# ScalarE normalises the odd head of each attention pair, and VectorE takes more of the prompt's rows beside it

## The chip, the cores and the metric

The kernel runs on one core of one Trainium2 chip. The metric is device time in microseconds (us) of one execution of the whole program. The core has TensorE (PE in the profile; its weight loads are PEld), VectorE (DVE), ScalarE (ACT), GpSimd (POOL) and SyncE (SP, whose queue starts most DMAs). Each engine works through its own instructions in the order in which they were written, and waits on semaphores for the others.

## The reference, cut to what matters

One encoder layer is applied to a prompt of 256 tokens and to a sample of 512 tokens. The change touches the self-attention of both, and moves work of the prompt's expert layer (`e_down[idx]` against the token) in time.

```python
N_HEADS, N_KV_HEADS, HEAD_DIM = 16, 4, 64

def block_attention(q, k, v):            # without a mask, over all S tokens
    ...
    s = jnp.einsum('bkgqd,bskd->bkgqs', q_blk, k).astype(jnp.float32) * scale
    p = jax.nn.softmax(s, axis=-1).astype(v.dtype)
    return jnp.einsum('bkgqs,bskd->bkgqd', p, v)

def peer_ffn(h, w_q, sub_k1, sub_k2, e_down, e_up):
    ...                                   # 8 heads x 16 experts for each token
    act = jax.nn.gelu(jnp.einsum('nhkd,nd->nhk', e_down[idx], xb))
    return jnp.einsum('nhk,nhkd->nd', g * act, e_up[idx])
```

## The kernel before, in words

The program handles the prompt first (2 tiles of 128 tokens), then the sample (4 tiles): projections of the mixer, self-attention, the mixer's outputs, cross-attention, the choice of experts (routing). After both come the experts. One block holds all stages up to the experts, so each engine runs from one stage into the next; what is shared between stages is handed over by semaphores.

**Self-attention** (`self_attention`) works on pairs of heads. A unit p is one pair of heads (even e = 0, odd e = 1) for one tile of 128 queries: N = 16 units for the prompt with w = 256 keys, N = 32 for the sample with w = 512. Each engine runs the same loop over steps, software-pipelined, and these are the instructions of step s:

- TensorE: `scores(s)` into `lin` (four banks, two per unit, so units s and s-2 share theirs); `turn(s-2)`, which transposes the normalised probabilities of both heads into two more banks of `lin`; `values(s-3)`, which multiplies the transposed probabilities by V into `tr`. `turn(p)` waits until both heads of p are normalised and until `copy` of unit p-1 has emptied the bank (`copied`).
- ScalarE: after every nt units (the last tile of a pair of heads) `T_hi <- tr` (L1000), then `copy(s-3)` (L992, two copies from PSUM into `att_probsT`), then `exp(s)` (L983, two exponentials with the bias `att_nmx` and the sum of each row, `att_rs`). `exp(s)` waits for the maxima of unit s.
- VectorE: `T_lo <- tr - T_hi` (L1021) where ScalarE made `T_hi`, the maxima of both heads of s in one reduction (L1026, `att_nmx`), then `norm(s-1)`: one reciprocal of both sums (L1011, `att_rr`) and one multiplication per head in place in `att_probs` (L1014, semaphore `normed`), then, in steps that are no multiple of 4, one background row.

The head-pair end falls on step 4k + 3 in the sample (k from 1) and on odd steps from 5 in the prompt. `att_probs` has three slots of two heads.

**Background rows** (`Rows`). The prompt's 256 rows of expert weights (one of 128 partitions x 1024 each) are gathered by GpSimd into `row_ring`, six slots (L148), and VectorE reduces each against the token (`tensor_tensor_reduce`, L136). VectorE takes a written number of them at written places of the sample's stages (`bg.dve(dve, n)`), in order; when the prompt is in its own attention there are none yet. In the sample's routing it takes 6, a weight split (`w_lo`, L189), 6, another split, and then `bg.finish` takes all that are left, before `pick_experts(0)` begins with L1729. GpSimd gathers a row as soon as its slot is free.

The scheduling is by hand: what an engine does next is the order in which the code above it was written.

Of the kernel before, what the change touches and what calls it, by code (L numbers as in the profile page):

```python
# [12 lines left out]
ALU = mybir.AluOpType  # L13
ACT = mybir.ActivationFunctionType
# [894 lines left out]
def self_attention(nc, block, q, bg, T, qT, kT, v_sb, ident, lin, tr, projected):  # L909

    with ExitStack() as ctx:
        m = Pool(nc, ctx)
        probs = m.sb("att_probs", [P, 3, 2, SAMPLE])
        pT = m.sb("att_probsT", [P, 2, 2, SAMPLE // P, P])
        nmx, rs, rr = (m.sb(f"att_{x}", [P, 3, 2]) for x in ("nmx", "rs", "rr"))
        scored, negated, exped, inverted, normed, turned, copied, valued, out_hi, out_lo = (
            m.sem(f"att_{x}") for x in ("scored", "negated", "exped", "inverted", "normed", "turned",
                                        "copied", "valued", "out_hi", "out_lo"))
        pairs = [(hp, t) for hp in range(NH // 2) for t in range(q.nt)]
        N, w = len(pairs), q.n  # L920
        kv_of = lambda hp: 2 * hp // (NH // NKV)
        rows_of = lambda e: slice(e * HD, (e + 1) * HD)
        block_end = [(hp + 1) * q.nt for hp in range(NH // 2)]

        @block.tensor
        def _(pe):
            def scores(p):

                hp, t = pairs[p]
                if p >= 2:  # L930
                    pe.wait_ge(exped, 2 * p - 2)
                for half in range(2):
                    cols = slice(half * w // 2, (half + 1) * w // 2)
                    for e in range(2):
                        last = pe.matmul(lin[:, 2 * (p % 2) + e, cols],
                                         qT[rows_of(e), hp, t * P:(t + 1) * P],
                                         kT[rows_of(e), kv_of(hp), cols],
                                         start=True, stop=True, skip_group_check=True)
                        if half == 1:
                            last.then_inc(scored, 1)  # L940

            def turn(p):
                for e in range(2):
                    pe.wait_ge(normed, 2 * p + e + 1)
                    if p >= 1:
                        pe.wait_ge(copied, 2 * p - 1 + e)
                    for kb in range(q.nt):
                        last = pe.transpose(lin[:, 4 + e, kb * P:(kb + 1) * P],
                                            probs[:, p % 3, e, kb * P:(kb + 1) * P], ident[:])
                    last.then_inc(turned, 1)  # L950

            def values(p):
                n, t = pairs[p]
                kv = kv_of(n)
                pe.wait_ge(copied, 2 * p + 2)
                if t == 0 and n >= 2:
                    pe.wait_ge(out_lo, n - 1)
                for kb in range(q.nt):
                    for e in range(2):
                        last = pe.matmul(tr[rows_of(e), n % 2, t * P:(t + 1) * P],  # L960
                                         v_sb[:, kb, kv * HD:(kv + 1) * HD], pT[:, p % 2, e, kb, :],
                                         start=(kb == 0), stop=(kb == q.nt - 1), skip_group_check=True)
                        if kb == q.nt - 1:
                            last.then_inc(valued, 1)

            projected(pe)
            for step in range(N + 3):
                if step < N:
                    scores(step)
                if 2 <= step < N + 2:  # L970
                    turn(step - 2)
                if 3 <= step:
                    values(step - 3)

        @block.scalar
        def _(act):
            def exp(p):
                i = p % 3
                act.wait_ge(negated, p + 1)
                for e in range(2):  # L980
                    if p >= 3:
                        act.wait_ge(turned, 2 * p - 5 + e)
                    act.activation(probs[:, i, e, 0:w], lin[:, 2 * (p % 2) + e, 0:w], ACT.Exp, bias=nmx[:, i, e:e + 1],  # L983
                                   accum_out=rs[:, i, e:e + 1]).then_inc(exped, 1)

            def copy(p):
                kbs = q.nt
                if p >= 2:
                    act.wait_ge(valued, 2 * p - 2)
                for e in range(2):  # L990
                    act.wait_ge(turned, 2 * p + e + 1)
                    act.activation(pT[:, p % 2, e, 0:kbs, :],  # L992
                                   lin[:, 4 + e, 0:kbs * P].rearrange("p (k q) -> p k q", k=kbs),
                                   ACT.Copy).then_inc(copied, 1)

            for step in range(N + 4):
                for n in range(NH // 2):
                    if step == block_end[n] + 3:
                        act.wait_ge(valued, 2 * block_end[n])
                        act.activation(T[0][:, n, 0:w], tr[:, n % 2, 0:w], ACT.Copy).then_inc(out_hi, 1)  # L1000
                if 3 <= step < N + 3:
                    copy(step - 3)
                if step < N:
                    exp(step)

        @block.vector
        def _(dve):
            def norm(p):
                i = p % 3
                dve.wait_ge(exped, 2 * p + 2)  # L1010
                dve.reciprocal(rr[:, i, :], rs[:, i, :]).then_inc(inverted, 1)  # L1011
                dve.wait_ge(inverted, p + 1)
                for e in range(2):
                    dve.tensor_scalar(probs[:, i, e, 0:w], probs[:, i, e, 0:w], rr[:, i, e:e + 1], None,  # L1014
                                      ALU.mult).then_inc(normed, 1)

            for step in range(N + 4):
                for n in range(NH // 2):
                    if step == block_end[n] + 3:
                        dve.wait_ge(out_hi, n + 1)  # L1020
                        dve.tensor_tensor(T[1][:, n, 0:w], tr[:, n % 2, 0:w], T[0][:, n, 0:w].bitcast(F32),  # L1021
                                          ALU.subtract).then_inc(out_lo, 1)
                if step < N:
                    i = step % 3
                    dve.wait_ge(scored, 2 * step + 2)
                    dve.tensor_reduce(nmx[:, i, :], lin[:, 2 * (step % 2):2 * (step % 2) + 2, 0:w], AX_X, ALU.max,  # L1026
                                      negate=True).then_inc(negated, 1)
                if 1 <= step < N + 1:
                    norm(step - 1)
                if step % 4 != 0:  # L1030
                    bg.dve(dve, 1)

        @block.gpsimd
        def _(pool):
            bg.pool(pool)

        def attended(eng):
            eng.wait_ge(out_lo, NH // 2)

        return attended  # L1040
# [1238 lines left out]
```

## Time and profile before

| | us |
|---|---|
| median of 3 runs | 2754.95 (2754.67 to 2755.43) |
| the profiled execution | 2751.85 |
| its span in the profile | 2749.9 |
| TensorE matmul busy | 2422.5 (88%) |
| VectorE busy | 2260.6 (82%) |
| ScalarE busy | 1103.4 (40%) |
| GpSimd busy | 1362.6 (50%) |
| self-attention of the prompt, about | 157 to 202 |
| self-attention of the sample, about | 777 to 895 |
| the last background row starts | 1368.2 |

A line of the timeline gives start, duration, engine, source line, what is written and read, and in brackets how long the engine had been idle before it and what ended that. Starts of successive instructions of one engine are closer than their durations, since they overlap. Two equal instructions in a row are merged into one line (x2) with their joint duration. Exponentials that also sum are followed by a short ACTIVATION_READ_ACCUMULATOR.

### The profile page before, as it was taken

Reading aid. Unit: us, or ns where it says so; the run is one execution under the profiler, and the core shown is the slowest. Engines: PE = TensorE matmul, PEld = TensorE weight load, DVE = VectorE, ACT = ScalarE, POOL = GpSimd, SP = SyncE. Lnnn points to the kernel's source line nnn. Section 1 sums busy time; section 2 is a strip of 40 time slices with the busy share of each in tenths; the row PEclk is TensorE's granted clock in tenths of the full one; section 3 lists DMA queues with packets and bytes.
Section 4 is the critical chain, followed back from the end, with each engine's and each line's share of the span. In section 5 each row is a group of like instructions: output and inputs, shape, how many; then the busy total and the mean of one; then the engine's idle time right before and its main releaser. Section 6 shows DMA issues by size and latency. Waiting matters only on the chain. (4 is left out here: it accounts for less than half of the span.)

```text
span 2749.9 us, 37781 instructions
## 1 busy us (share of the span) xinstructions
PE 2422.5 (88%) x12865; PEld 2096.2 (76%) x12865; DVE 2260.6 (82%) x3983; ACT 1103.4 (40%) x1934; POOL 1362.6 (50%) x1054
## 2 busy tenths in 40 slices
PE   6988989799989889889483668999999999999996
PEld 5766878677866667777373557999999999999996
DVE  6455436897788778876899997999999999999998
ACT  4453444333257223333125893333333333333333
POOL 0000000326632544644654346887777777777773
PEclk9999999899999999999797889999999999999998
DMA  4635444226963977866801359999999999999996
GB/s 159 203 116 194 154 153 138 68 86 231 354 239 117 342 275 269 321 237 221 316 31 62 131 207 365 403 415 414 405 404 401 402 400 400 406 403 394 411 402 225
DMA packets 231056, 747.57 MB, mean 272 GB/s; under 512 B 20864, under 2 KB 70064, under 8 KB 214288
## 3 DMA queue, kind: packets, MB, share of 16 engines
q0 software_dynamic: 112288, 408.77, 38.4%
q1 hardware_dynamic: 118640, 337.15, 33.4%
q8 instruction: 73, 1.20, 0.2%
q14 instruction: 55, 0.45, 0.0%
HBM read 708.09 MB, written 37.75 MB: 271 GB/s over the span
## 5 line engine op out<-in xcount | busy, mean ns | idle before, releaser
L148 POOL DMA_INDIRECT row_ring<-in_down,IDX x256 | 349.7, 1366 | 349.5 <-DVE dots L136 288.0
L189 DVE TENSOR_TENSOR w_lo<-w_raw,w_hi 128x2048 fp32r<-128x2048 f32 x116 | 267.3, 2305 | 241.5 <-ACT w_hi L183 238.3
L204 PE MATMUL lin<-w_hi,T_hi 128*128 128x512 f32 x976 | 393.2, 403 | 36.8 <-DVE w_lo L189 9.8
L205 PE MATMUL lin<-w_lo,T_hi 128*128 128x512 f32 x976 | 388.8, 398 | 0.0
L206 PE MATMUL lin<-w_hi,T_lo 128*128 128x512 f32 x976 | 388.7, 398 | 0.0
L183 ACT ACTIVATE w_hi<-w_raw 128x2048 fp32r<-128x2048 f32 x116 | 221.8, 1913 | 366.8 <-PE lin L206 341.7
L204 PE MATMUL tr<-T_hi,w_hi 128*128 128x384 f32 x1024 | 349.6, 341 | 9.8 <-DVE w_lo L2069 9.8
L136 DVE CUSTOM_DVE_ANT_0 row_ring<-row_ring,H 128x1024 f32<-128x1024 f32 x256 | 304.3, 1221 | 57.1 <-DMA row_ring<-in_down,IDX 54.7
L206 PE MATMUL tr<-T_hi,w_lo 128*128 128x384 f32 x1024 | 346.1, 338 | 0.0
L205 PE MATMUL tr<-T_lo,w_hi 128*128 128x384 f32 x1024 | 345.9, 338 | 0.0
L1988 POOL DMA_INDIRECT rows<-in_up,now x192 | 296.3, 1543 | 86.8 <-issue 50.6
L1988 POOL DMA_INDIRECT w_raw<-in_up,now x192 | 280.2, 1459 | 89.2 <-issue 47.4
L204 PE MATMUL lin<-w_hi,c_hi 128*128 128x512 f32 x768 | 300.3, 391 | 0.0
L205 PE MATMUL lin<-w_lo,c_hi 128*128 128x512 f32 x768 | 299.9, 391 | 0.0
L206 PE MATMUL lin<-w_hi,c_lo 128*128 128x512 f32 x768 | 299.0, 389 | 0.0
L204 PEld LDWEIGHTS lin<-w_hi,T_hi 128*128 128x128 f32 x976 | 186.0, 191 | 86.8 <-issue 15.2
L2032 ACT ACTIVATE w_hi<-row_ring 128x1024 fp32r<-128x1024 f32 x128 | 135.8, 1061 | 244.4 <-PE lin L206 242.3
L2040 ACT ACTIVATE gl<-tr 128x384 f32<-128x384 f32 x128 | 63.0, 492 | 396.2 <-PE tr L206 374.1
L204 PE MATMUL lin<-T_hi,w_hi 128*128 128x256 f32 (+1 forms) x512 | 174.0, 340 | 53.2 <-DVE w_lo L189 41.1
L206 PEld LDWEIGHTS lin<-w_hi,T_lo 128*128 128x128 f32 x976 | 186.0, 191 | 43.9
L205 PEld LDWEIGHTS lin<-w_lo,T_hi 128*128 128x128 f32 x976 | 186.4, 191 | 42.1
L204 PEld LDWEIGHTS tr<-T_hi,w_hi 128*128 128x128 f32 x1024 | 193.0, 189 | 14.9 <-DVE w_lo L2069 10.0
(284 smaller groups left out, 5284.9 us busy)
## 6 DMA issues: line engine op xcount, KB each, us to landing
w_raw<-in_wall SPq DMA_DIRECT2D x116, 1024.0 KB
G<-in_downT SPq DMA_DIRECT2D x128, 512.0 KB
row_ring<-in_up SPq DMA_DIRECT2D x128, 512.0 KB
wd<-dense_gates SPq DMA_DIRECT2D x32, 768.0 KB
dense_gates<-peer SPq DMA_DIRECT2D x6, 2048.0 KB, 7.2
dense_gates<-w_raw SPq DMA_DIRECT2D x6, 2048.0 KB, 6.5
row_ring<-in_down,IDX POOLq DMA_INDIRECT x256
Y<-in_x SPq DMA_DIRECT2D x6, 512.0 KB, 6.8
```

What stands on the lines that cost most here:

```text
L136: dve.tensor_tensor_reduce(self.ring[:, k, :], self.ring[:, k, :], self.H[:, r % 2, :], 1.0, 0.0, ALU.mult, ALU.add, self.dots[:, r:r + 1] ...
L148: pool.indirect_dma_start(self.ring[:, r % self.K, :], None, self.table, bass.IndirectOffsetOnAxis(ap=self.IDX[:, r:r + 1], axis=0)).then_ ...
L183: act.activation(self.hi[:, h % 2], self.raw[:, h % 2], ACT.Copy).then_inc(self.hi_done, 1)
L189: dve.tensor_tensor(self.lo[:, h % 2], self.raw[:, h % 2], self.hi[:, h % 2].bitcast(F32), ALU.subtract).then_inc(self.lo_done, 1)
L204: pe.matmul(out, lhs[0], rhs[0], start=start, stop=False, skip_group_check=True)
L205: pe.matmul(out, lhs[0], rhs[1], start=False, stop=False, skip_group_check=True)
L206: return pe.matmul(out, lhs[1], rhs[0], start=False, stop=stop, skip_group_check=True)
L1988: pool.indirect_dma_start(rows[k], None, table, bass.IndirectOffsetOnAxis(ap=now[:, j % 2, k:k + 1], axis=0)).then_inc(rows_in[k], 16)
L2032: act.activation(u_hi[:, b % 2], raw_u[:, b % RAW], ACT.Copy).then_inc(u_hid, 1)
L2040: act.activation(gl[:, b % 2, :], tr[:, b % 2, 0:DENSE], ACT.Gelu_apprx_tanh).then_inc(gelued, 1)
```

## The change

The even head's probabilities are still multiplied by VectorE. The odd head's are multiplied by ScalarE with an activation `Copy` whose scale is the column of `att_rr`, written at the end of ScalarE's step, for unit s-1. The semaphore `normed` becomes two, one for each head. VectorE takes a background row in all steps but the multiples of 8: 31 in the sample's attention in place of 27, so that `bg.finish` has four fewer.

```diff
-        scored, negated, exped, inverted, normed, turned, copied, valued, out_hi, out_lo = (
+        scored, negated, exped, inverted, normed_0, normed_1, turned, copied, valued, out_hi, out_lo = (
...
             def turn(p):
                 for e in range(2):
-                    pe.wait_ge(normed, 2 * p + e + 1)
+                    pe.wait_ge((normed_0, normed_1)[e], p + 1)
...
+            def norm_odd(p):
+                i = p % 3
+                act.wait_ge(inverted, p + 1)
+                act.activation(probs[:, i, 1, 0:w], probs[:, i, 1, 0:w], ACT.Copy,
+                               scale=rr[:, i, 1:2]).then_inc(normed_1, 1)
+
...
                 if step < N:
                     exp(step)
+                if 1 <= step < N + 1:
+                    norm_odd(step - 1)
...
-                for e in range(2):
-                    dve.tensor_scalar(probs[:, i, e, 0:w], probs[:, i, e, 0:w], rr[:, i, e:e + 1], None,
-                                      ALU.mult).then_inc(normed, 1)
+                dve.tensor_scalar(probs[:, i, 0, 0:w], probs[:, i, 0, 0:w], rr[:, i, 0:1], None,
+                                  ALU.mult).then_inc(normed_0, 1)
...
-                if step % 4 != 0:
+                if step % 8 != 0:
                     bg.dve(dve, 1)
```

On ScalarE, in the sample's attention around the end of a pair of heads (`T_hi`), this stands in a row before:

```order
L983 ACTIVATE att_probs_2,att_rs_2<-lin,att_nmx_2 128x512 x2
L1000 ACTIVATE T_hi<-tr 128x512
L992 ACTIVATE att_probsT_2<-lin 128x512 x2
L983 ACTIVATE att_probs_2,att_rs_2<-lin,att_nmx_2 128x512 x2
L992 ACTIVATE att_probsT_2<-lin 128x512 x2
```

And this now, where L998 and L1006 are the former L992 and L1000:

```order
L983 ACTIVATE att_probs_2,att_rs_2<-lin,att_nmx_2 128x512 x2
L989 ACTIVATE att_probs_2<-att_probs_2,att_rr_2 128x512
L1006 ACTIVATE T_hi<-tr 128x512
L998 ACTIVATE att_probsT_2<-lin 128x512 x2
L983 ACTIVATE att_probs_2,att_rs_2<-lin,att_nmx_2 128x512 x2
L989 ACTIVATE att_probs_2<-att_probs_2,att_rr_2 128x512
L998 ACTIVATE att_probsT_2<-lin 128x512 x2
```

Between the exponentials of one step and the copies of the next stands one more instruction.

On VectorE, at the same place, from `T_lo` on, before:

```order
L1021 TENSOR_TENSOR T_lo<-tr,T_hi 128x512
L1026 TENSOR_REDUCE att_nmx_2<-lin 128x2
L1011 RECIPROCAL att_rr_2<-att_rs_2 128x2
L1014 TENSOR_SCALAR att_probs_2<-att_probs_2,att_rr_2 128x512 x2
L136 ISA row_ring,dots<-row_ring,H 128x1024
L136 ISA dots 128x1
L1026 TENSOR_REDUCE att_nmx_2<-lin 128x2
L1011 RECIPROCAL att_rr_2<-att_rs_2 128x2
L1014 TENSOR_SCALAR att_probs_2<-att_probs_2,att_rr_2 128x512 x2
L1026 TENSOR_REDUCE att_nmx_2<-lin 128x2
```

And now, after a `T_lo` whose next step is a multiple of 4 but not of 8 (L1028, L1033, L1019 and L1021 are the former L1021, L1026, L1011 and L1014):

```order
L1028 TENSOR_TENSOR T_lo<-tr,T_hi 128x512
L1033 TENSOR_REDUCE att_nmx_2<-lin 128x2
L1019 RECIPROCAL att_rr_2<-att_rs_2 128x2
L1021 TENSOR_SCALAR att_probs_2<-att_probs_2,att_rr_2 128x512
L136 ISA row_ring,dots<-row_ring,H 128x1024
L136 ISA dots 128x1
L1033 TENSOR_REDUCE att_nmx_2<-lin 128x2
L1019 RECIPROCAL att_rr_2<-att_rs_2 128x2
L1021 TENSOR_SCALAR att_probs_2<-att_probs_2,att_rr_2 128x512
L136 ISA row_ring,dots<-row_ring,H 128x1024
L136 ISA dots 128x1
L1033 TENSOR_REDUCE att_nmx_2<-lin 128x2
```

One multiplication has gone from each step, and the step that had no row has one. TensorE's order is unchanged. GpSimd's gathers stand in the same order; 31 of them are written in the attention's part and 53 in the routing's, in place of 27 and 57.

## Rows read from the trace of the kernel before

**Rows 1.** Stretch, length; PE, PEld, DVE, ACT, POOL busy (instructions); clock, DMA share, GB/s.

```profile
193.00:199.00 6.00, 3.96 (x42) 2.58 (x40) 3.57 (x13) 4.14 (x16) 0.00 (x0) 1.00 0.01 3
800.00:840.00 40.00, 37.23 (x376) 27.55 (x374) 36.18 (x68) 30.04 (x75) 7.58 (x9) 1.00 0.39 120
```

**Rows 2.** Timeline of all engines, sample's attention, around one end of a head pair.

```profile
840.05 1.22 DVE L1026 TENSOR_REDUCE att_nmx<-lin 128x2 f32<-128x1024 f32 x1
...
842.65 0.60 ACT L1000 ACTIVATE T_hi<-tr 128x512 fp32r<-128x512 f32 x1
...
843.32 0.69 DVE L1021 TENSOR_TENSOR T_lo<-tr,T_hi 128x512 fp32r<-128x512 f32 x1
...
843.93 1.21 DVE L1026 TENSOR_REDUCE att_nmx<-lin 128x2 f32<-128x1024 f32 x1
...
845.17 0.69 ACT L983 ACTIVATE att_probs<-lin,att_nmx 128x512 f32<-128x512 f32 x1 [0.96 <-DVE att_nmx L1026]
845.25 0.89 DVE L1014 TENSOR_SCALAR att_probs<-att_probs,att_rr 128x512 f32<-128x512 f32 x2
...
845.85 0.68 ACT L983 ACTIVATE att_probs<-lin,att_nmx 128x512 f32<-128x512 f32 x1
...
846.04 1.22 DVE L136 CUSTOM_DVE_ANT_0 row_ring<-row_ring,H 128x1024 f32<-128x1024 f32 x1
...
846.51 1.08 ACT L992 ACTIVATE att_probsT<-lin 128x512 f32<-128x512 f32 x2
...
847.19 1.22 DVE L1026 TENSOR_REDUCE att_nmx<-lin 128x2 f32<-128x1024 f32 x1
847.22 0.91 PEld L948 LDWEIGHTS lin<-ident,att_probs 128*128 128x128 f32 x8 [0.54 <-issue]
...
848.29 1.09 PE L960 MATMUL tr<-att_probsT,v_sb 128*64 128x128 f32 x16
...
849.32 1.14 PE L935 MATMUL lin<-kT,G 64*128 64x256 f32 x8
...
850.53 1.22 DVE L1026 TENSOR_REDUCE att_nmx<-lin 128x2 f32<-128x1024 f32 x1 [1.13 <-PE lin L935]
```

**Rows 3.** The same timeline three ends of a head pair later.

```profile
884.57 0.69 DVE L1021 TENSOR_TENSOR T_lo<-tr,T_hi 128x512 fp32r<-128x512 f32 x1
```

**Rows 4.** Timeline of the prompt's attention, two ends of a head pair.

```profile
172.30 0.43 DVE L1021 TENSOR_TENSOR T_lo<-tr,T_hi 128x256 fp32r<-128x256 f32 x1 [0.64 <-ACT T_hi L1000]
...
174.79 0.68 PE L948 MATMUL lin<-ident,att_probs 128*128 128x128 f32 x4 [0.20 <-ACT att_probsT L992]
...
176.72 0.43 DVE L1021 TENSOR_TENSOR T_lo<-tr,T_hi 128x256 fp32r<-128x256 f32 x1 [0.64 <-ACT T_hi L1000]
```

**Rows 5.** ScalarE's groups by shape: count, busy us, mean ns, idle before.

```profile
L2046 ACT ACTIVATE c_hi<-gl 128x384 fp32r<-128x384 f32 x128 | 66.2, 517 | 40.6 <-DVE gl L2106 35.4 <-issue 5.0
L2040 ACT ACTIVATE gl<-tr 128x384 f32<-128x384 f32 x128 | 63.0, 492 | 396.2 <-PE tr L206 374.1 <-issue 22.1
...
L992 ACT ACTIVATE att_probsT<-lin 128x512 f32<-128x512 f32 x64 | 34.7, 601 | 1.4 <-PE lin L948 1.4
...
L285 ACT ACTIVATE T_hi<-lin,gains 128x512 fp32r<-128x512 f32 x24 | 15.4, 688 | 6.3 <-PE lin L277 6.2
```

**Rows 6.** Timeline of ScalarE: six activations with a scale column, back to back.

```profile
293.34 2.28 ACT L285 ACTIVATE T_hi<-lin,gains 128x256 fp32r<-128x256 f32 x6
```

**Rows 7.** Timeline of VectorE, GpSimd and TensorE at the end of the background rows.

```profile
1323.61 1.23 DVE L136 CUSTOM_DVE_ANT_0 row_ring<-row_ring,H 128x1024 f32<-128x1024 f32 x1 [3.19 <-DMA row_ring<-in_down,IDX]
...
1362.44 1.22 DVE L136 CUSTOM_DVE_ANT_0 row_ring<-row_ring,H 128x1024 f32<-128x1024 f32 x1
...
1368.21 1.23 DVE L136 CUSTOM_DVE_ANT_0 row_ring<-row_ring,H 128x1024 f32<-128x1024 f32 x1
...
1362.16 0.94 POOL L148 DMA_INDIRECT row_ring<-in_down,IDX  x1 [0.30 <-issue]
...
1376.91 0.80 PE L204 MATMUL lin<-T_hi,w_hi 128*128 128x512 f32 x1 [41.10 <-DVE w_lo L189]
```

More of the change, by code:

```diff
@@ L915, in self_attention @@
         nmx, rs, rr = (m.sb(f"att_{x}", [P, 3, 2]) for x in ("nmx", "rs", "rr"))
-        scored, negated, exped, inverted, normed, turned, copied, valued, out_hi, out_lo = (
-            m.sem(f"att_{x}") for x in ("scored", "negated", "exped", "inverted", "normed", "turned",
+        scored, negated, exped, inverted, normed_0, normed_1, turned, copied, valued, out_hi, out_lo = (
+            m.sem(f"att_{x}") for x in ("scored", "negated", "exped", "inverted", "normed_even", "normed_odd", "turned",
                                         "copied", "valued", "out_hi", "out_lo"))
```

## The prediction

> **What bounds the kernel now.** I read the page for the stages, then the busy time of the two attention stretches, then the timeline of a few steps, since the shares alone mislead here. In the sample's attention TensorE is busy 37.23 of 40 us, VectorE 36.18, ScalarE 30.04 [rows 1]. That looks like a race between TensorE and VectorE with ScalarE at leisure. The timeline says who is late. Follow one unit from its maxima at 843.93 [rows 2]: the first exponential starts at 845.17 (+1.24), the second at 845.85 (+0.68), the copies at 846.51 (+0.66), TensorE's transposes at 847.22 (+0.71), the values at 848.29 (+1.07), the scores at 849.32 (+1.03), the maxima two steps later at 850.53 (+1.21). The sum is 6.60 us for two steps, 3.30 a step. Nothing in this ring waits for anything outside it: the transposes cannot begin before the copy of the preceding unit has emptied their bank, and the scores stand behind transposes and values in TensorE's order. VectorE sat idle 1.13 us before the maxima at 850.53. So the limit of a plain step is a **latency ring through all three engines**, and ScalarE's stretch from the first exponential to the copy is a part of it, though ScalarE itself idles 0.96 us before the exponential at 845.17.
>
> At the end of a head pair, `T_hi` stands before the copies on ScalarE and `T_lo` before the maxima on VectorE: from the maxima at 840.05 to those at 843.93 it is 3.88 us, namely 2.60 to `T_hi`, 0.67 to `T_lo`, 0.61 to the maxima [rows 2]. With VectorE's full step behind it (843.93 to 847.19, 3.26), four steps are 3.88 + 3.26 + 6.60 = 13.74. Measured over three such blocks: (884.57 - 843.32) / 3 = 13.75 [rows 2, 3]. The account closes. Without VectorE's limit at 847.19 the ring alone would have given 840.05 + 6.60 + 0.47 (for `T_hi`, which delays the copies by the spacing of one copy) = 847.12, so VectorE costs 0.07 us in four steps.
>
> The prompt's attention has the same ring with half the keys: 176.72 - 172.30 = 4.42 us for two steps, each with one end of a head pair, and there too the transposes are released by a copy [rows 4].
>
> **The change, part by part.**
> *The activation added on ScalarE.* It stands behind the exponentials of unit s and ahead of the copies of unit s-2, thus in the ring, once in each turn of two steps. It waits for the reciprocal, which VectorE gives right behind the maxima (the multiplication that needs it starts 845.25 - 843.93 = 1.32 after them), while the activation's turn comes 1.24 + 0.68 + 0.66 = 2.58 us after: no wait. Its cost is its spacing. Two copies from PSUM of 601 ns take 1.08 together, so the overlap is 0.12 [rows 2, 5]. With a scale column the same shape takes 688 ns [rows 5]. Reading SBUF in place of PSUM adds about 517 - 492 = 25 ns [rows 5]. 0.688 + 0.025 - 0.12 = 0.59, and an instruction with a column behind an exponential starts 0.02 later than a plain one (0.68 against 0.66): x = 0.61 us. At 256 wide: six with a column take 2.28 in all, with the same overlap (2.28 - 0.12) / 6 = 0.36 apart [rows 6]; with 0.025 and 0.02, x' = 0.40. Bounds: below, the plain copy's spacing of 0.48, that is 0.13 less, and 0.27 for x'; above, no overlap at all, 0.688 + 0.025 = 0.71, that is 0.10 more, and 0.50 for x'.
>
> *Sample.* The first activation in front of a copy is that of step 1 or 2. The maxima of step 4 come x later, those of step 6 2x, those of step 7, the first end of a head pair, 3x. From there to the end at step 31 are six blocks of four steps. A block holds two turns of the ring in a row (each 3.88 and each 6.60 becomes longer by x), and loses VectorE's 0.07, since VectorE's step is shorter by a multiplication: 2x - 0.07 = 1.15. Behind step 31 the exponentials are followed by one more activation ahead of a copy (x); the last activation falls into a gap, at about 0.1. Sum: 3x + 6 (2x - 0.07) + x + 0.1 = 16x - 0.32 = **+9.4 us**, between 7.4 and 11.0.
>
> *Prompt.* The first copy that TensorE waits for and that is delayed is the one behind unit 2's exponentials; from there each turn of two steps costs x', up to step 15 seven of them, and one in the tail: 8x' = **+3.2 us**, between 2.2 and 4.0.
>
> *The multiplication removed on VectorE.* It is 0.40 us a step (845.25 to 846.04 is 0.79 for two). VectorE was idle or bound at 0.07 in four steps, which is counted. Worth nothing else.
>
> *Four more rows in the sample's attention.* One row is 1.15 us (846.04 to 847.19) [rows 2], in the steps behind the ends of a head pair, where the ring is slowest. There VectorE has from the maxima to the next ones 3.26 - 1.15 = 2.11 us of work without a row, and 3.26 - 0.40 = 2.86 with one multiplication less and a row; the step itself took 850.53 - 847.19 = 3.34 and gets longer. Hidden. If the step were VectorE's they would cost 2.86 - 2.11 = 0.75 each, 3.0 in all.
>
> *Four fewer rows in `bg.finish`.* There TensorE idles 41.10 us until VectorE has made the weight split behind the rows [rows 7], so each row removed counts. Before it are 38 rows: five are there already, then 33 run from 1323.61 to 1368.21, which is 44.60 / 32 = 1.39 a row, more than the 1.15 of VectorE, because a gather is issued only every 0.94 + 0.30 us and now and then later [rows 7]. Four rows: 5.6 us. Bounds: 4 x 1.15 = 4.6, and the last four's own 1368.21 - 1362.44 = 5.8. I take **-5.6 us**, the pace of the stretch.
>
> *Waits and queues.* Behind the new activation stand only ScalarE's copies; both semaphores of the heads are met before the copies that `turn` also waits for. GpSimd's gathers move with the rows; the weight loads on SyncE's queue have their buffers filled long before attention ends. 0.
>
> The sum: 9.4 + 3.2 - 5.6 = +7.0 us. Against the profiled execution that is 2751.85 + 7.0 = 2758.9; the median lies 3.1 us above that execution, so 2754.95 + 7.0 = **2762.0 us**. With the bounds: lowest 7.4 + 2.2 - 5.8 = +3.8 (2758.8), highest 11.0 + 4.0 - 4.6 = +10.4 (2765.4).
>
> **The rivals.**
> *A, ScalarE's idle time hides the activation.* ScalarE waits 0.96 us before an exponential [rows 2], more than x. If the copies had slack, only the rows would count: -5.6, 2749.3 us. It decides on whether TensorE's transposes follow the copies: 846.51 to 847.22 is one copy and a semaphore, and in the prompt 0.20 us of TensorE's wait is put to the copy by name [rows 4]. The idle time lies ahead of the exponentials, the activation behind them. 8%.
>
> *B, VectorE is the bound, and its relief sets the pace.* VectorE busy 36.18 of 40 us [rows 1] speaks for it, the idle 1.13 us against it. If each step followed VectorE, the prompt would gain about 16 x 0.27 = 4.3 and the sample 32 x 0.40 = 12.8 less TensorE's floor: scores, transposes and values take about 1.14 + 1.07 + 1.03 = 3.24 [rows 2], so no more than (13.75 - 4 x 3.24) x 8 = 6.3. With the rows: -4.3 - 6.3 - 5.6 = -16.2, 2738.8 us. 3%. The Trainium skill, "Perfetto Trace Analysis" (Optimizing Scalar/DVE Operations), says that moving work from a saturated VectorE to ScalarE may make sense; that is this rival. Its page "ScalarE: Activation LUTs" (Rules for kernel authors) says the reverse, that multiplications belong on VectorE. By the first the time would be B's 2738.8, by the second it rises; the trace agrees with the second, with 0.40 us for a multiplication on VectorE against 0.61 worked out above, and a VectorE that waits.
>
> *C, the rows' time is not given back.* Something else, GpSimd's gathers at the head of the routing, could end `bg.finish` at the same distance. Then +12.6, 2767.6 us. Against it: the gathers run on without a pause but for their own issue up to 1362.16 [rows 7]. 6%.
>
> *D, TensorE's longer waits cost clock.* The granted clock is 1.00, the 2.4 GHz level, at 37.23 busy of 40, but also at 3.96 of 6 in the prompt's end [rows 1], so 0.3 us more idle a step should not matter. If for a turn it fell to the lower level, TensorE's 3.24 a step would double: some 3 us a step, a few steps, +20 in all: about 2775. 3%.
>
> **How the numbers follow.** The forecast (the ring grows by x in each turn, four rows are given back) has 80%, from 2758.8 to 2765.4. C at 6% makes 86%, so the range is 2758 to 2768; A, B and D stay out. A measurement of this kernel tells some 0.2% (5.5 us) from no change. The forecast lies 1.5 us past that bound: of its 80% I put 62 above it and 18 below; with C and D slower has 71%. A straddles the bound on the other side (-0.2%): 4 to same, 4 to faster, which with B is 7%. Same: 22%.
>
> **What would show it.** In the sample's attention the distance of two `T_lo` is 14.9 us in place of 13.75, in the prompt's 4.82 in place of 4.42. The new activation lasts about 0.71 (512) and about 0.50 (256), and the copies start 0.61 later behind the exponentials, the transposes still 0.71 behind the copies; TensorE's wait before them grows to about 0.8. VectorE's idle time before the maxima grows. `bg.finish` has 34 rows, and from its first row to L1729 5.6 us less. The forecast is wrong if the transposes start where they did, if the activation takes above 0.8, or if the rows in `bg.finish` run at another pace.

## The result, and the profile after

The changed kernel takes 2761.9 us (median; 2754.09 to 2768.24) against 2754.44 us (2745.45 to 2757.98) for the kernel before, timed in turn with it. The ratio is 1.0029, with the 95% interval 1.0021 to 1.0038: slower by about 7.5 us. In a later comparison it was 1.0027 (1.0016 to 1.0039; run e5). The forecast was 2762.0 us. The profiled execution of the changed kernel took 2760.21 us.

The page of the changed kernel, its span and the busy time of the engines:

```profile
span 2758.3 us, 37781 instructions
PE 2424.5 (88%) x12865; PEld 2096.2 (76%) x12865; DVE 2245.5 (81%) x3935; ACT 1128.7 (41%) x1982; POOL 1356.3 (49%) x1054
```

ScalarE has 25 us more work and VectorE 15 us less, TensorE's is the same. The time followed neither sum, so the shares don't explain it.

ScalarE's groups by shape (count, busy us, mean ns, idle before), the new activation and the copies that stand behind it, to be put beside [rows 5]:

```profile
L998 ACT ACTIVATE att_probsT<-lin 128x512 f32<-128x512 f32 x64 | 34.7, 600 | 0.9 <-PE lin L948 0.9
L989 ACT ACTIVATE att_probs<-att_probs,att_rr 128x512 f32<-128x512 f32 x32 | 23.0, 717 | 0.0
...
L989 ACT ACTIVATE att_probs<-att_probs,att_rr 128x256 f32<-128x256 f32 x16 | 8.1, 504 | 0.0
```

The new activation lasts 717 and 504 ns and never waits. The timeline of all engines in the sample's attention shows one turn of the ring, as [rows 2] does for before:

```profile
844.20 1.23 DVE L1033 TENSOR_REDUCE att_nmx<-lin 128x2 f32<-128x1024 f32 x1 [0.32 <-PE lin L935]
...
848.14 1.22 DVE L1033 TENSOR_REDUCE att_nmx<-lin 128x2 f32<-128x1024 f32 x1 [2.13 <-PE lin L935]
...
849.40 0.69 ACT L983 ACTIVATE att_probs<-lin,att_nmx 128x512 f32<-128x512 f32 x1 [0.91 <-DVE att_nmx L1033]
...
850.08 0.68 ACT L983 ACTIVATE att_probs<-lin,att_nmx 128x512 f32<-128x512 f32 x1
...
850.74 0.72 ACT L989 ACTIVATE att_probs<-att_probs,att_rr 128x512 f32<-128x512 f32 x1
...
851.35 1.08 ACT L998 ACTIVATE att_probsT<-lin 128x512 f32<-128x512 f32 x2
...
851.42 1.22 DVE L1033 TENSOR_REDUCE att_nmx<-lin 128x2 f32<-128x1024 f32 x1 [0.32 <-PE lin L935]
...
852.09 1.12 PE L948 MATMUL lin<-ident,att_probs 128*128 128x128 f32 x8 [0.74 <-ACT att_probsT L998]
...
855.26 0.69 DVE L1028 TENSOR_TENSOR T_lo<-tr,T_hi 128x512 fp32r<-128x512 f32 x1 [0.87 <-ACT T_hi L1006]
```

From the exponential at 850.08 to the new activation it is 0.66 us, from there to the copies 0.61, from the copies to the transposes 0.74, which wait for nothing else: the step that read 0.66 in [rows 2] is now 0.66 + 0.61. From the maxima at 844.20 to those at 851.42 it is 7.22 us for two steps, where it was 6.60. VectorE was idle 2.13 us ahead of the maxima at 848.14 and ScalarE still 0.91 us ahead of the exponential at 849.40. The stretch from 800 to 840, to be put beside [rows 1] (length; PE, PEld, DVE, ACT, POOL busy; clock, DMA share, GB/s):

```profile
800.00:840.00 40.00, 34.40 (x350) 25.73 (x348) 31.59 (x55) 33.57 (x78) 8.79 (x10) 1.00 0.42 132
```

TensorE, VectorE and ScalarE are idle 5.6, 8.4 and 6.4 of 40 us. No engine is full, and the added instruction was still paid in full.

`bg.finish` has four rows less. What this document calls the rows' stretch runs on VectorE from the multiplication L1706 (L1713 in the changed kernel) to the first MAX8 behind the last row. Its first 25.6 to 25.8 us, in all twelve traces of this case, are twelve rows and two weight splits ahead of `bg.finish`; the rest is `bg.finish`. VectorE's timeline of the changed kernel, the head of this stretch, its last row, and what follows:

```profile
1305.68 1.22 DVE L1713 TENSOR_TENSOR H<-G,pairs 128x1024 f32<-128x1024 f32 x1
...
1377.68 1.22 DVE L136 CUSTOM_DVE_ANT_0 row_ring<-row_ring,H 128x1024 f32<-128x1024 f32 x1
...
1378.84 0.86 DVE L1736 MAX8 best<-G 128x8 f32<-128x128 f32 x4
```

TensorE's wait behind it, which was 41.10 us in [rows 7]:

```profile
1386.38 0.79 PE L204 MATMUL lin<-T_hi,w_hi 128*128 128x512 f32 x1 [35.38 <-DVE w_lo L189]
```

The wait is only 5.7 us shorter where the stretch is 7.4 shorter, because TensorE began to wait 1.7 us sooner, counted from L1706 or L1713 (45.3 us behind it in place of 47.0). What ends the wait is VectorE, so the length of its stretch is the measure.

The same stretches in both traces. "Middle" is from the first to the sixth `T_lo` of the prompt's attention, from the first to the seventh of the sample's; head and tail are from the first maxima and to the last `T_lo`.

| us | before | after | moved | forecast |
|---|---|---|---|---|
| prompt, head / middle / tail | 10.54 / 22.13 / 7.01 | 11.53 / 24.13 / 9.26 | +5.2 | +3.2 |
| sample, head / middle / tail | 21.40 / 82.50 / 10.25 | 23.19 / 89.64 / 10.31 | +9.0 | +9.4 |
| rows' stretch (L1706 or L1713 to MAX8) | 80.60 | 73.16 | -7.4 | -5.6 |
| all the rest | | | +1.6 | 0 |
| span | 2749.9 | 2758.3 | +8.4 | +7.0 |

### The profile page after: what moved, and what is told of

It reads as the page before. It is cut to its first block and busy times, and to the rows that moved or that the text cites. A ratio compares the mean times of both kernels' runs of the same rounds, so it can differ in the third digit from the quotient of the medians.

```text
span 2758.3 us, 37781 instructions
## 1 busy us (share of the span) xinstructions
PE 2424.5 (88%) x12865; PEld 2096.2 (76%) x12865; DVE 2245.5 (81%) x3935; ACT 1128.7 (41%) x1982; POOL 1356.3 (49%) x1054
```

## Experiments

Two theories stood against each other. **The ring**: what counts is that the activation stands between the exponentials and the copies; four more rows in attention are free. **The load**: ScalarE, or the new dependence of TensorE on ScalarE's multiplication, costs the time wherever the instruction stands, or (for the rows) VectorE is close to its limit. All runs were compared with the kernel before on their own chip: e1 to e4 on one, e5 to e8 on a second, e9 and e10 on a third.

### e1 and e2: the two parts apart

Only the rows, in the kernel before:

```diff
-                if step % 4 != 0:
+                if step % 8 != 0:
                     bg.dve(dve, 1)
```

> The kernel before with only the background rows moved (VectorE takes one in all steps but the multiples of 8; both heads stay on VectorE). My account: the four added rows fall into steps where the ring gives VectorE 3.34 us for 3.26 us of work, so the distance of two T_lo in the sample's attention stays 13.75 us (at most 13.9), and the end of the background rows comes 5.6 us sooner (the changed kernel's trace says up to 7.4): about 2749 us, ratio 0.998. If VectorE were the bound of attention, four steps would get 0.8 us or more longer: 2752. If the rows' time were not given back in bg.finish: 2754.4.

Only the odd head, the changed kernel with the rows of before:

```diff
-                if step % 8 != 0:
+                if step % 4 != 0:
                     bg.dve(dve, 1)
```

> The changed kernel with the rows as before (none in the multiples of 4): the odd head on ScalarE alone. The ring account: +12.6 us (9.4 in the sample's attention, 3.2 in the prompt's), 2767 us, ratio 1.0046; T_lo 14.94 us apart in the sample and 4.83 in the prompt. If the cost of the changed kernel lay in the moved rows and the activation were hidden in ScalarE's idle time: 2754.4. If the granted clock in the prompt's tail falls with it, as in the one profile of the changed kernel, 2 to 3 us more: 2769.

| | us | ratio to before (95%) | prompt middle | sample middle | rows' stretch |
|---|---|---|---|---|---|
| before, in the same comparison | 2752.78 | | | | |
| e1, rows | 2744.42 | 0.9969 (0.9958 to 0.998) | 22.14 | 82.50 | 75.15 |
| e2, odd head | 2765.56 | 1.0056 (1.0042 to 1.007) | 24.13 | 89.65 | 80.58 |

The kernel is slower by one part and faster by the other: +12.8 us and -8.4 us. The rows alone leave both attentions as they were; the odd head alone has all of the lengthening and none of the gain. In e1's profile the rows' stretch is 5.5 us shorter than before (75.15 against 80.60), less than the 8.4 of the medians. Their sum, +4.4, is 3 us under the +7.5 of the whole; each figure carries 3 to 4 us of its own (the intervals), so this is no contradiction and no confirmation of the last microseconds.

### e3 and e6: the same instruction at two places, with nobody reading its result

The kernel before gets one more activation per step. It scales V by a column of `ident` into a tile that nothing reads, so it computes something in excess and the attention waits for none of its results. In e3 it stands behind the exponentials, where the changed kernel has its activation; in e6 ahead of them:

```diff
+            def more(p):
+                if p >= 1:
+                    act.wait_ge(extra_done, p)
+                act.activation(extra[:, 0:w // 256, :], v_sb[:, 0:w // 256, :], ACT.Copy,
+                               scale=ident[:, 0:1]).then_inc(extra_done, 1)
...
                 if step < N:
                     exp(step)
+                if 1 <= step < N + 1:
+                    more(step - 1)
```

> The kernel before, and one activation more on ScalarE in each step, of the same size and with a scale column, which reads v_sb and writes a tile that nobody reads; it stands behind the exponentials, in front of the next copies. Nothing waits for its result. The ring account: the place alone costs, 0.61 us in each turn of two steps (512 wide) and 0.40 (256 wide): T_lo 14.97 us apart, 2767 us, ratio 1.0047, as with the odd head moved. If it is the dependence of TensorE on the odd head's result that costs, and ScalarE's idle 0.96 us a step hides a mere activation: 13.75 us apart, 2754.4.

```diff
+                if 1 <= step < N + 1:
+                    more(step - 1)
                 if step < N:
                     exp(step)
-                if 1 <= step < N + 1:
-                    more(step - 1)
```

> As the extra activation in the ring (kernel before, result unused, same size, scale column), but in front of the exponentials of a step, where ScalarE waits for the maxima. The ring account: the 0.96 us of idle take 0.61 us; T_lo 13.75 us apart in the sample (at most 13.9), 4.43 in the prompt, total as before within 2 us. If the number of instructions on ScalarE counts and not the place: 14.94 us apart and 13 to 14 us slower, as in the ring.

| | us | ratio to before (95%) | prompt middle | sample middle |
|---|---|---|---|---|
| e3, behind the exponentials | 2766.72 | 1.0052 (1.0039 to 1.0066) | 24.13 | 89.64 |
| e6, ahead of them | 2753.3 | 1.0007 (0.9998 to 1.0016) | 22.15 | 82.50 |

ScalarE's timeline in e3:

```profile
846.23 0.68 ACT L984 ACTIVATE att_probs<-lin,att_nmx 128x512 f32<-128x512 f32 x1
...
846.89 0.71 ACT L990 ACTIVATE att_extra<-v_sb,ident 128x512 bf16<-128x512 f32 x1
847.51 1.08 ACT L999 ACTIVATE att_probsT<-lin 128x512 f32<-128x512 f32 x2
849.50 0.69 ACT L984 ACTIVATE att_probs<-lin,att_nmx 128x512 f32<-128x512 f32 x1 [0.91 <-DVE att_nmx L1035]
```

And in e6, at the same place of a block:

```profile
846.22 0.68 ACT L984 ACTIVATE att_probs<-lin,att_nmx 128x512 f32<-128x512 f32 x1
...
846.88 1.08 ACT L999 ACTIVATE att_probsT<-lin 128x512 f32<-128x512 f32 x2
847.83 0.74 ACT L990 ACTIVATE att_extra<-v_sb,ident 128x512 bf16<-128x512 f32 x1
848.81 0.69 ACT L984 ACTIVATE att_probs<-lin,att_nmx 128x512 f32<-128x512 f32 x1 [0.24 <-DVE att_nmx L1035]
```

In e3 the copies start 1.28 us after the second exponential and the idle time ahead of the next exponential is 0.91; in e6 they start 0.66 after it, as in [rows 2], and the activation has gone into the idle time, of which 0.24 is left. The middle of the sample's attention is 89.64 in e3, exactly that of the changed kernel, although no one waits for the extra result. So it is the **place in ScalarE's order** that costs, neither ScalarE's sum of work nor the dependence. Beside its own kernel before, e3 costs 13.9 us (2766.72 - 2752.78) and e6 2.0 (2753.3 - 2751.28), with an interval that holds zero.

### e4: the changed kernel with its activation in the gap

Here ScalarE still scales the odd head, but ahead of the exponentials. The reciprocal has to be there earlier, so VectorE makes it ahead of `T_lo` and the maxima:

```diff
+                if 2 <= step < N + 1:
+                    norm_odd(step - 1)
                 if step < N:
                     exp(step)
-                if 1 <= step < N + 1:
-                    norm_odd(step - 1)
+                if step == 1:
+                    norm_odd(0)
...
             for step in range(N + 4):
+                if 2 <= step < N + 1:
+                    invert(step - 1)
```

> The changed kernel with the odd head's activation in front of the exponentials of a step, where ScalarE waits for the maxima, in place of behind them; for this VectorE takes the reciprocal of unit s-1 ahead of the maxima of unit s. Same instructions, other places. The ring account: ScalarE's idle 0.96 us a step takes the 0.61, the ring is back at 6.60 us: T_lo 13.7 us apart (at most 14.0), and the four rows are won: 2748.5 us (2746 to 2751), ratio 0.998. If ScalarE's sum of work is what costs, wherever it stands: 14.9 us apart and 2762 as the changed kernel.

2745.92 us, ratio 0.9976 (0.9967 to 0.9985). Prompt's middle 22.16, sample's 82.34, rows' stretch 74.22. The timeline of all engines:

```profile
846.02 1.08 ACT L998 ACTIVATE att_probsT<-lin 128x512 f32<-128x512 f32 x2
...
846.16 0.17 DVE L1021 RECIPROCAL att_rr<-att_rs 128x2 f32<-128x2 f32 x1
...
846.70 1.23 DVE L1040 TENSOR_REDUCE att_nmx<-lin 128x2 f32<-128x1024 f32 x1 [0.37 <-PE lin L935]
...
846.97 0.74 ACT L989 ACTIVATE att_probs<-att_probs,att_rr 128x512 f32<-128x512 f32 x1
...
847.96 0.69 ACT L983 ACTIVATE att_probs<-lin,att_nmx 128x512 f32<-128x512 f32 x1 [0.25 <-DVE att_nmx L1040]
```

The same arithmetic on the same engines, with the activation moved ahead of two exponentials and the reciprocal ahead of the maxima, is some 14 us faster than the changed kernel (0.9976 against 1.0029 and 1.0027). All that the change cost is regained. But e4 is no faster than e1, which leaves the odd head on VectorE and moves only the rows (0.9976 against 0.9969): in the whole time the move of the odd head itself is worth nothing, and in the sample's middle 0.2 us (82.34 against 82.50).

### e5: the changed kernel once more

It ran on the chip of e6 to e8 and shows which parts of the first trace recur.

> The changed kernel once more, beside the others on the same chip. 7 to 8 us above before (ratio 1.0029 and its interval). Sample's T_lo 14.94 us apart, prompt's 4.83. Three profiles of kernels with the activation in the ring each show the granted clock fall to its lower level in a tail of attention (prompt or sample), three without it none: if the longer waits of TensorE bring that about, this profile shows such a fall too; if it is chance, it need not.

2759.16 us against 2751.28, ratio 1.0027 (1.0016 to 1.0039). Both middles are those of the first trace to 0.01 us (24.13 and 89.64). The rows' stretch took 75.12 in place of 73.16, the prompt's tail 8.52 in place of 9.26: these two vary from one execution to the next.

### e7 and e8: what is the relief of VectorE good for?

If moving the odd head frees VectorE, more rows should fit. Both take a row in every step but the first, which leaves 30 for `bg.finish`: e7 in e4, e8 in the kernel before, where VectorE has both multiplications. The edit of e7 (in e8 the line was `step % 4 != 0`):

```diff
-                if step % 8 != 0:
+                if step != 0:
                     bg.dve(dve, 1)
```

> The odd head's activation in front of the exponentials as before, and VectorE takes a background row in all steps of the sample's attention but the first: 35 rows in attention, 30 left for bg.finish in place of 34. VectorE has 2.86 us of work in a step of 3.3, so T_lo stay 13.7 us apart; bg.finish gives back 4 x 1.39 = 5.6 us by the pace in its rows, 6.7 by the difference measured between 38 and 34 rows: 5.6 to 6.7 us under the kernel with 34, about 2739 to 2740. If attention has no more room: as that one, 2746.

> The kernel before (both heads on VectorE) with a background row in all steps but the first: VectorE's work is then 3.26 us in each plain step against a ring of 3.30, and 3.88 + 3.26 + 6.60 = 13.74 stays the sum of four steps. The ring account: T_lo 13.75 us apart (at most 13.9), bg.finish 5.6 to 6.7 us shorter than with 34 rows: about 2738 to 2740 us; then the odd head's move buys nothing at all. If VectorE is the bound from here on and the removed multiplication is what makes room: T_lo 14.2 or more apart, 2742 or more, above the kernel with the activation in the gap.

| | us | ratio to before (95%) | sample middle | rows' stretch |
|---|---|---|---|---|
| e7, odd head on ScalarE | 2740.67 | 0.9962 (0.9948 to 0.9976) | 82.29 | 69.03 |
| e8, both heads on VectorE | 2739.59 | 0.996 (0.9946 to 0.9975) | 82.52 | 69.62 |

The two tie: all rows fit beside both multiplications. VectorE's timeline in e8, two plain steps up to the end of a head pair:

```profile
846.98 1.23 DVE L1026 TENSOR_REDUCE att_nmx<-lin 128x2 f32<-128x1024 f32 x1
...
850.26 1.22 DVE L1026 TENSOR_REDUCE att_nmx<-lin 128x2 f32<-128x1024 f32 x1
...
853.53 0.69 DVE L1021 TENSOR_TENSOR T_lo<-tr,T_hi 128x512 fp32r<-128x512 f32 x1
```

No idle time stands ahead of any of them; a step with everything in it is 850.26 - 846.98 = 3.28 us, against the ring's 3.30. The stretch from 800 to 840 in e8:

```profile
800.00:840.00 40.00, 37.52 (x378) 27.72 (x376) 39.58 (x75) 29.89 (x74) 10.34 (x11) 1.00 0.53 155
```

VectorE is busy 39.58 of 40 us and still costs nothing, because its own work and the ring come out at the same length.

### e9 and e10: shorten the ring at the head pair's end

A head pair's end costs the ring 0.47 us, because `T_hi` stands ahead of the copies. Moved behind them (and `T_lo` behind the maxima and `norm`), it should leave the ring; then VectorE's own sum decides, and the relief of VectorE could count for the first time. e9 is e7 with this, e10 is e8 with this. On ScalarE:

```diff
             for step in range(N + 4):
+                if 3 <= step < N + 3:
+                    copy(step - 3)
                 for n in range(NH // 2):
                     if step == block_end[n] + 3:
                         act.wait_ge(valued, 2 * block_end[n])
                         act.activation(T[0][:, n, 0:w], tr[:, n % 2, 0:w], ACT.Copy).then_inc(out_hi, 1)
-                if 3 <= step < N + 3:
-                    copy(step - 3)
```

> The kernel with the odd head's activation ahead of the exponentials and rows in all steps but the first, and T_hi behind the copies on ScalarE, T_lo behind the maxima and the multiplication on VectorE: both out of the ring, into waiting time. The ring account: the 0.47 of T_hi and the 0.61 that T_lo adds to the maxima go; VectorE has 4 x 2.86 + 0.61 = 12.05 us of work in four steps, ScalarE's gap of 0.96 is overfull by about 0.1 once in four: T_lo 13.3 to 13.5 us apart in the sample's attention, 4.17 to 4.25 in the prompt's (4.43 now), 4 to 5 us under the same kernel without this move (2740.7): about 2736. If the ends of head pairs are not in the ring: no change, 13.7 and 4.43.

> The kernel before with rows in all steps but the first and the same move of T_hi and T_lo, both heads still on VectorE. Now VectorE has 4 x 3.26 + 0.61 = 13.65 us of work in four steps of the sample, more than the ring's 13.2: VectorE becomes the bound, T_lo 13.65 us apart, and only the prompt gains (4.17 to 4.25 in place of 4.43; some 2 us): about 2737.5. The difference to the kernel with the odd head on ScalarE, 0.2 to 0.3 us in four steps, is what its move is worth once the ring is shorter. If VectorE is not the bound here either: 13.2 us apart, 2735.

| | us | ratio to before (95%) | prompt, two steps | sample, four steps |
|---|---|---|---|---|
| before, in the same comparison | 2752.65 | | 4.426 | 13.75 |
| e9, odd head on ScalarE | 2738.21 | 0.9946 (0.9934 to 0.9957) | 4.214 | 13.295 |
| e10, both heads on VectorE | 2735.81 | 0.9943 (0.9931 to 0.9956) | 4.154 | 13.753 |

(The steps are from the traces, the means of the middle. In e9 the prompt's first turn is 4.45 and the next four are 4.16 each.) VectorE's timeline in e10:

```profile
842.10 0.69 DVE L1028 TENSOR_TENSOR T_lo<-tr,T_hi 128x512 fp32r<-128x512 f32 x1
842.70 1.22 DVE L136 CUSTOM_DVE_ANT_0 row_ring<-row_ring,H 128x1024 f32<-128x1024 f32 x1
...
843.84 1.22 DVE L1021 TENSOR_REDUCE att_nmx<-lin 128x2 f32<-128x1024 f32 x1
```

The stretch from 800 to 840 in e10:

```profile
800.00:840.00 40.00, 37.16 (x376) 27.46 (x372) 39.57 (x75) 29.64 (x74) 10.38 (x11) 1.00 0.52 154
```

The same in e9:

```profile
800.00:840.00 40.00, 38.45 (x385) 28.64 (x386) 36.15 (x64) 37.76 (x88) 11.50 (x13) 1.00 0.55 159
```

In e10 VectorE is busy 39.57 of 40 us: now it is the bound, and the sample's block stays at 13.75, where 13.65 was expected. The same share in e8 was no cost, because there the ring was as long as VectorE's work; here the ring is shorter. In e9, with a multiplication less on VectorE, the block is 13.295, 0.46 shorter. That is the only place in this study where the relief of VectorE shows by more than 0.04 us a block (13.72 in e4 and 13.71 in e7, against 13.75). In the six middle blocks it is 2.75 us. The medians do not show it: e9 is not faster than e10 (2738.21 against 2735.81, intervals overlapping almost wholly). In their traces e9's attention of the sample is 1.9 us shorter in all, head and tail included, and that of the prompt 0.8 longer. Both are faster than both kernels of this case. e10, with the odd head left on VectorE, is the simplest of them.

## Why the prediction was right, step by step

**What bounds the kernel.** Shown. The ring that [rows 2] gave as 6.60 us for two steps became 7.22, by the one instruction put into it, while VectorE's idle time grew; e3 lengthened it alike with an instruction that nobody waits for, and e6 did not with the same instruction 1 us further on.

**The added activation, x.** 0.61 us forecast, 0.61 between the activation and the copies in the rows above. A ring of two steps grew by 0.62, and the distance of two `T_lo` by 1.19 (855.26 less the one before it):

```profile
840.32 0.69 DVE L1028 TENSOR_TENSOR T_lo<-tr,T_hi 128x512 fp32r<-128x512 f32 x1 [0.88 <-ACT T_hi L1006]
```

855.26 - 840.32 = 14.94 against 13.75, where 1.15 was forecast. The forecast took off 0.07 a block for VectorE's limit; with a multiplication less and no added ring e4 and e7 lost only 0.03 and 0.04 (13.72 and 13.71 against 13.75), which is the difference. Over the six blocks that is +7.14 (89.64 - 82.50) against 6.90. The duration of 717 ns against 0.688 + 0.025 = 713 shows that the price from other rows of the same engine was sound. The Trainium skill, "ScalarE: Activation LUTs" (What ACT_TABLE_LOAD costs), gives 186 ns + 0.833 ns an element, 93 ns more for a pointer operand, and an overlap of 93 ns; that is an estimate of 705 ns, 612 apart. This trace agrees, with 717 ns and 0.61 us apart.

**x'.** 0.40 forecast. The prompt's middle grew by 2.00 us in five turns, 0.40 each.

**Sample.** +9.4 forecast, +9.0 in the profiles. The head gave 1.79 (3x = 1.83), the tail 0.06, where x was forecast: the before trace's own tail of 10.25 was long, since e1 and e8 have 9.69, and against these the tail of 10.31 is x longer (0.62).

**Prompt.** +3.2 forecast, +5.2 in the two profiles. Here a rival took part. Head and middle have about what was forecast (0.99 and 2.00 for 7 x 0.40 = 2.8). A head alone says little, since it varies with the granted clock. The ten us from the first maxima on (columns as above) in before, changed kernel, e6 and e3:

```profile
161.76:171.76 10.00, 8.18 (x60) 6.24 (x60) 6.20 (x18) 5.85 (x23) 0.00 (x0) 0.66 0.38 137
162.24:172.24 10.00, 7.77 (x46) 5.74 (x48) 4.99 (x14) 6.52 (x24) 0.00 (x0) 0.56 0.40 147
161.72:171.72 10.00, 7.57 (x62) 5.66 (x62) 6.78 (x20) 8.56 (x32) 0.00 (x0) 0.72 0.39 143
162.24:172.24 10.00, 7.26 (x60) 5.25 (x60) 6.21 (x18) 7.89 (x30) 0.00 (x0) 0.74 0.38 134
```

The heads are 10.54, 11.53, 9.42 and 10.09 us. At nearly the same clock the longer ring of e3 costs the head 0.67 beside e6, near two turns of x' (0.80), so some 0.3 of the 0.99 would be the clock; that is an estimate from these four. The tail took 9.26, where e2 has 7.40 with the same ring. The windows of the changed kernel tell why (columns as above):

```profile
199.00:202.00 3.00, 1.77 (x16) 1.15 (x18) 0.88 (x3) 2.31 (x8) 0.00 (x0) 0.82 0.03 5
202.00:205.00 3.00, 2.12 (x16) 1.42 (x14) 0.42 (x1) 1.50 (x5) 0.00 (x0) 0.50 0.00 0
205.00:208.00 3.00, 2.03 (x17) 1.63 (x14) 0.43 (x1) 0.57 (x2) 0.12 (x1) 0.50 0.00 0
```

The granted clock went to the lower level, 1.2 GHz, for the last microseconds of the prompt's attention. This is rival D at another place and a tenth of its price: not a turn of the ring at half speed for 20 us, but 1 to 2 us in a tail. It is discussed below.

**The multiplication removed from VectorE, and four more rows in attention.** 0 forecast for both; e1 leaves the sample's middle at 82.50, e4 at 82.34.

**Four fewer rows in `bg.finish`.** -5.6 forecast, -7.4 in the two profiles, -5.5 in e1's profile, -8.4 in the medians of e1, with an interval from -11.6 to -5.5. This is the term that was sized least well. Its step took the mean pace of the stretch, 1.39 us a row, and that pace held: from the sixth row of `bg.finish` to the last it is (1377.68 - 1339.21) / 28 = 1.37 in the changed kernel. Of the 7.4 us, 6.1 lie between these rows (44.60 in [rows 7] against 38.47). Another 1.1 is a wait ahead of them. The first five rows of `bg.finish` are there when VectorE comes to them, and for the sixth it waits in all twelve traces, by 2.1 to 3.3 us. Before it was 3.19 [rows 7], in the changed kernel 2.08:

```profile
1339.21 1.23 DVE L136 CUSTOM_DVE_ANT_0 row_ring<-row_ring,H 128x1024 f32<-128x1024 f32 x1 [2.08 <-DMA row_ring<-in_down,IDX]
```

In e5, the same kernel, it is 3.32, so the shorter wait belongs to this execution and not to the change. The rows' stretch is 80.87 on average with 38 rows (80.58 to 81.43 in four kernels), 74.41 with 34 (73.16 to 75.15 in four) and 69.48 with 30 (69.03 to 70.03 in four): 6.5 us for the first four and 4.9 for the next, 1.42 a row over the eight. The pace forecast is thus right over eight rows; for these four it was 0.9 short. Since the traces with 34 rows alone lie up to 2.0 us apart, 6.5 and 4.9 may be the same number, and no cause for a difference is shown.

**The sum.** The two errors, about 1 to 2 us too little for the prompt and about 1 too little for the rows' gain, have opposite signs. The median of +7.5 lies 0.5 from +7.0 partly for that reason. That 2762.0 and 2761.9 differ by 0.1 is luck: the base of the sum, 2754.95, came from three runs, and twenty gave 2754.44. What the runs bear out is the pair of large terms: forecast +12.6 and -5.6, measured apart +12.8 and -8.4.

**The rivals.** A (idle time hides the activation) is refuted by e3 and holds where it was not meant: in e6 the same idle time does hide it, since there the instruction lies in it. B (VectorE is the bound) is refuted by e1 and by e8, which load VectorE more at no price; it becomes true only in e10, once the ring is shorter. (e3, with both multiplications on VectorE, has the sample's middle of the changed kernel, 89.64, so their number doesn't matter beside the longer ring either.) The Trainium skill's advice in "Perfetto Trace Analysis" (Optimizing Scalar/DVE Operations), to move work from a saturated VectorE to ScalarE, bought nothing in the whole time here, neither where the rows alone had VectorE busy 37.30 of 40 us (e1, with e4 beside it) nor with 39.58 (e8, with e7 beside it); only e9's steps show more than 0.04 us a block of VectorE's relief. C (rows not given back) is refuted by e1. D occurred in a small form.

## What to carry to other kernels

Ask of an added instruction in which interval of its engine's order it stands, and follow the timeline from one loop-carried event to the same event a turn later: idle time helps only the instruction that stands in it, and here moving one activation past two exponentials was worth 12 to 14 us. When a change joins a gain and a loss, measure the parts apart; the rows alone gave 0.9969 where both together gave 1.0029. A high busy share alone doesn't make an engine the bound: VectorE at 90% of the stretch before still waited 1.13 us ahead of the maxima at 850.53 [rows 2], and at 99% it cost nothing in e8, where the ring was as long, and 0.46 us a block in e10, where the ring was shorter.

## What the runs showed of the hardware

**The granted clock falls in the tails of attention in some executions.** In six of the twelve traces (before, after, and e1 to e10) the granted clock reads 0.50 for some microseconds at the end of an attention: prompt's end in after, e3, e5, e6 and e7, the sample's in e2. The windows of e6 and of e2 at that place; e6:

```profile
196.00:199.00 3.00, 2.13 (x18) 1.30 (x18) 0.65 (x2) 1.69 (x6) 0.00 (x0) 0.85 0.00 0
199.00:202.00 3.00, 2.03 (x17) 1.63 (x18) 0.42 (x1) 0.70 (x2) 0.00 (x0) 0.50 0.00 0
```

e2:

```profile
901.00:904.00 3.00, 3.00 (x23) 2.67 (x22) 0.64 (x2) 0.81 (x3) 2.40 (x2) 0.50 0.75 208
```

And e4, where it doesn't fall, though TensorE was busy less in the same microseconds:

```profile
196.00:199.00 3.00, 1.37 (x13) 0.95 (x14) 0.95 (x3) 2.18 (x8) 0.00 (x0) 1.00 0.00 0
199.00:202.00 3.00, 2.03 (x21) 1.36 (x22) 0.42 (x1) 1.08 (x4) 0.01 (x1) 1.00 0.00 0
```

It costs 1 to 2 us: the prompt's tail is 7.0 in kernels with the ring of before, 8.0 with the fall (e6, e7); 7.40 with the longer ring (e2), 8.5 and 9.3 with the fall (e3 and e5, after); the sample's 10.31, and 11.92 in e2. All four traces with the longer ring have it, and two of the eight others. That would fit TensorE's longer waits making it likelier, but so few traces don't show it, and it stays open whether a part of the measured +7.5 us comes by this way. At the heads the lower level is no exception: all twelve traces have it for 7 to 10 us around the first steps of the prompt's attention and for 3 to 7 in the sample's. From 800 to 840, the middle of the sample's attention, the clock is 1.00 in all twelve.

**The spread.** Executions of one kernel on one chip spread by 10 us and more (the kernel before by 16 us in one comparison). In kernels with the same steps the middle of the sample's attention recurs to 0.02 us. The spread lies elsewhere. The most of it is between the two attentions, from the prompt's last `T_lo` to the sample's first maxima: 574.9 us in e1, 575.8 in e8, 579.2 before, 580.1 after, 582.4 in e3, although no edit touches that stretch. The rest is in the prompt's head (9.4 to 11.5 us in these traces), in the tails, between the sample's attention and L1706 (392.2 to 397.8), in the rows' stretch and in what comes after it (1378.4 to 1380.5). The +1.6 us of "all the rest" in the first comparison is well within this. The difference between e1's -8.4 and its -5.5 in the rows' stretch may come from there too: in e1's trace the stretch between the attentions was 4.3 us shorter than before. A term of a few tenths per turn is therefore read from the trace better than from the medians.
